# Residual additions of a two-block transformer kernel: matmul results copied to SBUF by ScalarE first, then added by VectorE

## The reference

```python
# first block, two layers
n = rms_norm(h, attn_norm[l])
h = h + mixer(n, ...) @ w_out
h = h + conv_glu_ffn(rms_norm(h, ffn_norm[l]), ...)      # ... @ w_down
# second block, two layers
h = layer_norm(DN_ALPHA * h + token_mixers(h, ...) @ w_out, ln1_g[l], ln1_b[l])
h = layer_norm(DN_ALPHA * h + conv_ffn(h, ...) @ w_down, ln2_g[l], ln2_b[l])
```

## Time and profile before

| | |
|---|---|
| time, median of 3 runs | 2877.43 us (2876.21 to 2878.27) |
| the profiled execution's own time | 2877.43 us |
| its span, first to last instruction | 2875.4 us |
| TensorE busy | 2709.6 us, 94% |
| VectorE busy | 1725.8 us, 60% |
| ScalarE busy | 1005.6 us, 35% |
| GpSimd busy | 1020.5 us, 35% |
| mean granted TensorE clock | 0.964 of full speed |

### The profile page before, as it was taken

One profiled execution on the slowest core, in us unless ns is written; L12 is line 12 of the kernel. 1 busy time (PEld: TensorE's weight loads), 2 busy tenths in 40 slices (PEclk: granted clock), 3 DMA queues, 4 the chain that ended last, 5 costly groups with the idle time before them and its releaser, 6 DMA issues.

```text
span 2875.4 us, 34500 instructions
## 1 busy us (share of the span) xinstructions
PE 2709.6 (94%) x11434; PEld 1997.4 (69%) x11434; DVE 1725.8 (60%) x2250; ACT 1005.6 (35%) x1548; POOL 1020.5 (35%) x383
## 2 busy tenths in 40 slices
PE   8999999999998999999698998999989998899998
PEld 6654788888764678888475455788767644687876
DVE  3645774575486576377559336827634943583682
ACT  3344322232144242232442434323344334432332
POOL 2210344444321244444144123444424411344452
PEclk9997999999998899999899999999999998999999
DMA  4110223232211123223111011222221110122221
GB/s 152 59 45 23 73 95 102 90 103 86 81 52 37 45 94 102 89 95 102 45 54 52 30 39 64 97 93 95 98 71 59 47 44 23 66 95 96 94 99 69
DMA packets 56404, 212.15 MB, mean 74 GB/s; under 512 B 6400, under 2 KB 6656, under 8 KB 56192
## 3 DMA queue, kind: packets, MB, share of 16 engines
q1 hardware_dynamic: 55456, 209.60, 21.6%
q10 hardware_dynamic: 864, 1.44, 0.2%
HBM read 208.92 MB, written 2.10 MB: 73 GB/s over the span
## 4 chain that ended last, share of the span: by engine, by line
PE 75%; DVE 11%; ACT 5%; issue 5%; POOL 3%; DVEq 1%; ACTq 0%; DMA 0%; POOLq 0%; SPq 0%
PE bank_G L499 21%; PE bank_G L501 20%; PE bank_G L500 20%; PE bank_S L1128 4%; POOL wlo L447 3%; PE bank_O L1138 2%; DVE conv_up L751 2%; PE bank_X L1148 2%; DVE mx L2025 1%; PE bank_S L546 1%; PE bank_X L1693 1%; ACT whi L472 1%; DVE prod L771 1%; PE bank_X L820 1%; DVE scores_t L1671 1%
## 5 line engine op out<-in xcount | busy, mean ns | idle before, releaser
L447 POOL TENSOR_TENSOR wlo<-raw,whi 128x1024 fp32r<-128x1024 f32 (+1 forms) x361 | 977.7, 2709 | 1726.6 <-ACT whi L472 1726.6
L499 PE MATMUL bank_G<-n_hi,whi 128*128 128x512 f32 x2392 | 974.8, 408 | 62.5 <-DVE n_lo L606 24.7
L501 PE MATMUL bank_G<-n_hi,wlo 128*128 128x512 f32 x2392 | 942.2, 394 | 0.0
L500 PE MATMUL bank_G<-n_lo,whi 128*128 128x512 f32 x2392 | 942.0, 394 | 0.0
L472 ACT ACTIVATE whi<-raw 128x1024 fp32r<-128x1024 f32 (+1 forms) x363 | 404.3, 1114 | 825.4 <-PE bank_G L501 825.3
L499 PEld LDWEIGHTS bank_G<-n_hi,whi 128*128 128x128 f32 x2392 | 456.4, 191 | 203.4 <-issue 59.1
L501 PEld LDWEIGHTS bank_G<-n_hi,wlo 128*128 128x128 f32 x2392 | 455.3, 190 | 98.7
L500 PEld LDWEIGHTS bank_G<-n_lo,whi 128*128 128x128 f32 x2392 | 456.8, 191 | 95.8 <-issue 7.7
L666 DVE SCALAR_TENSOR_TENSOR h<-h,bank_G 128x512 f32 (+1 forms) x96 | 66.0, 688 | 393.1 <-PE bank_G L501 393.1
L499 PE MATMUL bank_G<-a_hi,whi 128*128 128x512 f32 x704 | 275.3, 391 | 5.8 <-DVE a_lo L773 3.6
L500 PE MATMUL bank_G<-a_lo,whi 128*128 128x512 f32 x704 | 274.0, 389 | 0.0
(11 more groups left out here) (270 smaller groups left out, 2552.2 us busy)
## 6 DMA issues: line engine op xcount, KB each, us to landing
raw<-in_w_mix_in SPq DMA_DIRECT2D x42, 512.0 KB, 3.2
raw<-in_w_out SPq DMA_DIRECT2D x32, 512.0 KB, 3.2
raw<-in_w_hyb_in SPq DMA_DIRECT2D x25, 512.0 KB, 3.2
raw<-in_w_diff_in SPq DMA_DIRECT2D x24, 512.0 KB, 3.2
raw<-in_w_up0a SPq DMA_DIRECT2D x22, 512.0 KB, 3.2
raw<-in_w_up0b SPq DMA_DIRECT2D x22, 512.0 KB, 3.2
raw<-in_w_up1a SPq DMA_DIRECT2D x22, 512.0 KB, 3.2
raw<-in_w_up1b SPq DMA_DIRECT2D x22, 512.0 KB, 3.2
```

Source lines behind the costliest of these rows:

```text
L447: pool.tensor_tensor(b.wlo[:, g.slot, 0:width], b.raw[:, g.slot, 0:width], b.whi[:, g.slot, 0:width], ALU.subtract).then_inc(b.lo_ready, 1)
L499: pe.matmul(out, b.whi[:, g.slot, w], hi[:, k, :], start=(k == 0), stop=False)
L500: pe.matmul(out, b.whi[:, g.slot, w], lo[:, k, :], start=False, stop=False)
L501: mm = pe.matmul(out, b.wlo[:, g.slot, w], hi[:, k, :], start=False, stop=(k == pieces - 1))
```

## The change

ScalarE now empties the bank in the residual groups as well: `products_act` calls `take` (a copy of the bank to `mixed`, a buffer of two 128x512 tiles in SBUF, and behind it `split_hi`) where it had called `split_hi`. VectorE's addition reads `mixed` in the bank's place, waits for `evacuated` in place of `gemm_done`, and signals a new semaphore `resid_done`. The copy into a half of `mixed` waits until the addition two tiles before has read it. Waits on `evacuated` that had meant "h is updated" become waits on `resid_done`, the eight gained copies behind out0 and out1 each wait for their own tile in place of the last, and two waits that ScalarE had at the start of groups, for all of the preceding group to be evacuated, go.

```diff
-def products_act(act, b, name, gain=None):
+def products_act(act, b, name, r0, gain=None):
     g0, tiles = group_tiles(name)
     width = WIDTH[g0]
     if gain:
         for k in range(tiles):
-            split_hi(act, b, Index(g0 + k + 2))
+            wait(act, b.resid_done, r0 + k - 1 if k else max(r0 - 1, 0))
+            take(act, b, Index(g0 + k), b.mixed[:, (g0 + k) % 2, :])
             if k and not name.startswith("out"):
-                act.wait_ge(b.evacuated, g0 + k)
+                act.wait_ge(b.resid_done, r0 + k)
                 gained_hi_act(act, b, gain, k - 1)
 
         for k in range(0 if name.startswith("out") else tiles - 1, tiles):
-            act.wait_ge(b.evacuated, g0 + (tiles if name.startswith("out") else k + 1))
+            act.wait_ge(b.resid_done, r0 + k + 1)
             gained_hi_act(act, b, gain, k)
         return
 
-    for i, g, g_next in pairs(act, g0, tiles - 2):
-        split_hi(act, b, g.after(2), width)
-        split_hi(act, b, g_next.after(2), width)
-    split_hi(act, b, Index(g0 + tiles))
-    split_hi(act, b, Index(g0 + tiles + 1))
+    def one(g, r, w=None):
+        wait(act, b.resid_done, r)
+        take(act, b, g, b.mixed[:, g.slot, :], width=w)
+
+    one(Index(g0), max(r0 - 1, 0))
+    one(Index(g0 + 1), r0)
+    for i, g, g_next in pairs(act, g0 + 2, tiles - 4):
+        one(g, r0 + 1 + 2 * i, width)
+        one(g_next, r0 + 2 + 2 * i, width)
+    one(Index(g0 + tiles - 2), r0 + tiles - 3)
+    one(Index(g0 + tiles - 1), r0 + tiles - 2)
@@ products_dve @@
-    def one(g, h, last=False):
-        dve.wait_ge(b.gemm_done, g.at(1))
-        dve.scalar_tensor_tensor(h, h, float(alpha), b.G[:, g.slot, :], ALU.mult, ALU.add).then_inc(b.evacuated, 1)
+    def one(g, h, r, last=False):
+        dve.wait_ge(b.evacuated, g.at(1))
+        ins = dve.scalar_tensor_tensor(h, h, float(alpha), b.mixed[:, g.slot, :], ALU.mult, ALU.add).then_inc(b.resid_done, 1)
         if stats == "square":
-            dve.wait_ge(b.evacuated, g.at(1))
+            dve.wait_ge(b.resid_done, r)
             link(dve.tensor_tensor(b.sq[:, 0, :], h, h, ALU.mult))
         if last:
             if stats == "sum":
-                dve.wait_ge(b.evacuated, g.at(1))
+                dve.wait_ge(b.resid_done, r)
             dve.sem_inc(b.last_ready, 1)
         elif stats:
-            dve.wait_ge(b.evacuated, g.at(1))
+            dve.wait_ge(b.resid_done, r)
...
@@ ffn_up_act @@
-    if not scaled:
-        act.wait_ge(b.evacuated, g0)
```

More of the change, by code:

```diff
@@ L305, in allocate @@
     b.nlo_ready = sem("nlo_ready")
+    b.resid_done = sem("resid_done")
     b.conv_done = sem("conv_done")
@@ L681, in products_dve @@
                 dve.sem_inc(b.acc_ready, 1)
-            one(Index(g0 + k), b.h[:, k, :], last=k == tiles - 1)
+            one(Index(g0 + k), b.h[:, k, :], RES[name] + k + 1, last=k == tiles - 1)
             if k and not name.startswith("out"):
@@ L691, in products_dve @@
         for s, x in enumerate((g, g_next)):
-            one(x, b.h[:, bass.ds(2 * i + s, 1), :].rearrange("p a t -> p (a t)"))
+            one(x, b.h[:, bass.ds(2 * i + s, 1), :].rearrange("p a t -> p (a t)"), RES[name] + 1 + s + 2 * i)
     link.end(looped // 2)
     if stats:
-        one(Index(g0 + tiles - 2), b.h[:, tiles - 2, :])
+        one(Index(g0 + tiles - 2), b.h[:, tiles - 2, :], RES[name] + tiles - 1)
         dve.sem_inc(b.acc_ready, 1)
-        one(Index(g0 + tiles - 1), b.h[:, tiles - 1, :], last=True)
+        one(Index(g0 + tiles - 1), b.h[:, tiles - 1, :], RES[name] + tiles, last=True)
+RES = {}
+for _n in range(4):
+    RES.update({f"out{_n}": 24 * _n, f"down{_n}a": 24 * _n + 8, f"down{_n}b": 24 * _n + 16})
 def ffn_up_pe(pe, b, name, nlo):
@@ L787, in ffn_act @@
         ffn_up_act(act, b, f"up{f}{tag}", FC * f + HC * half)
-        products_act(act, b, f"down{f}{tag}", gain if half else None)
+        products_act(act, b, f"down{f}{tag}", RES[f"down{f}{tag}"], gain if half else None)
 def ffn_dve(dve, b, link, f, stats, gain=None, nhi=0):
@@ L2245, in _ @@
             hyb_attention_act(act, b)
-            products_act(act, b, "out0", "ffn_norm0")
+            products_act(act, b, "out0", RES["out0"], "ffn_norm0")
             rms_scale_act(act, b, link, 1)
@@ L2252, in _ @@
             diff_attention_act(act, b, link)
-            products_act(act, b, "out1", "ffn_norm1")
+            products_act(act, b, "out1", RES["out1"], "ffn_norm1")
             rms_scale_act(act, b, link, 3)
@@ L2261, in _ @@
                 mixer_act(act, b, link, l, mixw)
-                products_act(act, b, f"out{2 + l}")
+                products_act(act, b, f"out{2 + l}", RES[f"out{2 + l}"])
                 layer_norm_act(act, b, link, 6 + 2 * l, f"ln1_b{l}", 64 + 24 * l, True)
```

## The result

The changed kernel takes 2891.8 us (median of 4 executions, 2888.1 to 2892.9) where the kernel before takes 2876.8 beside it (2872.4 to 2878.3): ratio 1.0053 [1.0037, 1.0069], 15 us slower. A repetition gave 2891.75 against 2876.0, the same ratio. The forecast was 2884.6, 2880.5 to 2891.5: right in direction, less than half of the size. The profiled execution of after takes 2890.4 us, its span 2888.4 at a mean granted clock of 0.961; before it was 2875.4 at 0.964.

A forecast was written before the change was run, and what follows sets the result against it. The prediction saw TensorE bound by its product tiles, plus chains over other engines where it waits. Delays at eight ends and three starts summed to 7.15 us on 2877.4, giving 2884.6, range 2880.5 to 2891.5.

The forecast's parts named there:

- The view of the kernel: Copies inside runs of product tiles cost nothing; only those in chains over other engines that TensorE waits for cost time.
- The direct sum: Delays at group ends and starts, 1.52 + 0.76 + 1.60 + 1.47 + 1.80 = 7.15 us, without any clock term.
- The handover at the ends: Gap from ScalarE's copy to VectorE's operation at group ends, taken as 0.04 us; 0.16 was the upper bound.
- an end of the first kind: Ends of down0b, down1b and down3b, 0.76 us later each; ends of out0 and out1, 0.80 each.
- the ends with a mean: Ends of out2, down2b and out3: POOL's split holds the first centring, 0.49 us later each, 1.47 in all.
- the starts: Third tile of out1, out2 and out3, where TensorE waits for wlo: 0.6 us later each, 1.8 in all.
- TensorE's wait at out0's end: Sign that the forecast is right: this wait grows from 1.67 to about 2.5 us in the profile after.
- a split inside a run: POOL's weight split in out1 had 1.8 us to spare; 1.3 would be left after the copy.
- The order of VectorE and POOL: At the ends VectorE's square still starts before POOL's split, by 0.27 us, or 0.15 with the long handover.
- The rival in which the square loses: At ends of down0b, down1b, out0 and out1 the square waits behind POOL's split: 13.7 us, 2891.1; chance 0.12.
- The clock: Low-clock TensorE stretches behind waits: taken as zero, with the range widened, more upward; one or two stretches are 2 to 4 us.
- A count of low-clock stretches that differs by more than two: Sign that the forecast is wrong, to be read in the profile after.

The follow-up runs named there:

- both direct: Changed kernel, but the first two tiles of the out groups and the last tile before each norm added straight from the bank: 2874.32 us, ratio 0.9993 to before.
- shifted kernels: Changed kernel with two or four extra memsets ahead of the first weight split, shifting it by 1.3 or 2.6 us: 2888.18 and 2889.56 us.
- Halves: Changed kernel with only the last tiles before norms, or only the out groups' first two tiles, added straight from the bank: 2889.16 and 2887.53 us.
- single places: "both direct" with the copy back at block 1's ends, block 2's ends, out2's start or out3's start alone: 2881.62, 2882.49, 2878.62, 2882.97 us.
- bridging: A few unread TensorE products put into the waits that the change lengthens: changed kernel 2888.95 us (1.0044), kernel before 2874.16 us (0.9987).

## Why the forecast was right in direction and wrong in size

**The view of the kernel** held: a copy inside a run is free ("both direct" makes 80 and is not slower), and only the places where ScalarE or VectorE stand directly between two products pay.

**The direct sum** held. Forecast 7.15, bounds 5.4 to 8.5; the trace's gaps give 6.7, the rest apart from the clock +7.2 +- 0.9, and doubling the copy doubles it. Its small errors: the addition takes 0.69, not 0.75; the row that it was taken from has a per-partition scalar (`vec`) where this one has a constant. That is 0.06 too much at five places. The handover at the ends is 0.03 (taken as 0.04). So an end of the first kind costs 0.70 (forecast 0.76 and 0.80), the ends with a mean 0.48 (0.49), the starts 0.62 (0.6). Of the signs that were named, TensorE's wait at out0's end did not go to 2.5 but stayed at 1.67, with the growth in the wait before it; and a split inside a run has 1.07 us to spare, not 1.3.

**The order of VectorE and POOL** was called right: the square starts 0.35 ahead of the split at down0b's end (forecast 0.27) and takes 0.69. The rival in which the square loses gives 2891.1, which is nearly the measured time, and is still wrong: its long squares don't exist, as all 32 take 691 to 695 ns. A number that fits is no evidence for its mechanism.

**The clock** is the step that failed: "I leave it at nothing and widen the range". It is +8.0 +- 1.4 us, as much as the direct sum. Neither reason for leaving it at nothing carried that far. The first was that such a stretch "comes or doesn't come after nearly the same wait", so that longer waits make it only "a little more likely". That holds for the pair of the earlier trace rows, but the start of out2 turned from never to always when its wait went from 1.2 to 1.9. The second was that three executions within 2.1 us meant that the sum evens out. Scatter within a kernel says nothing on a shift of its mean, and three were few: 102 executions reach over 15 us. "A count of low-clock stretches that differs by more than two" was named as a sign against the forecast, and it came: 33 and 36.

**What stays open.** The slow third tiles of out2 and out3 are some 3.2 us of lost time and are explained by the idling ahead of them. For the remaining 4 to 5 us of the clock part no cause is shown. In the two traces of after the largest piece, 4.6 us, lies between down2b's end and out3, partly in a mixer without a copy, and it is gone in the traces of the shifted kernels. Halves and single places each have a clock part whose sum exceeds the whole; bridging lowers both kernels alike; a shift takes off a little. Also unexplained is the rest of "both direct", -2.0 +- 0.9, against which the rests of the four single places add up to 11.8, where the trace's gaps make 5.5 (with 0.12 off at each of the five ends of the first kind); so the parting into clock part and rest is good to a few us, not better.

## What to carry to other kernels

An operation put between a product and its consumer is free inside a pipelined run and costs its full length, plus handover, where the engines take turns: count these places and read one of each kind. Then ask what the longer wait does to TensorE's clock on the products behind it; when a kernel waits for a microsecond or two at many places, such a lengthening can cost as much again, as it did here, and it deserves a term with a positive expectation, not zero. Where a wait can't be removed, a few cheap products on data that are ready anyway can pay for themselves (0.13% here, with 18 of them). 111 of them cost 6 us.

## What the hardware showed that I had not expected

- Low-clock time is worth 0.31 us of span per us over whole executions, but in out2's third tile 0.47: mean clock 0.76 over 7.0 us is 3.4 us at the lower level, and 1.6 were lost. The Trainium skill (TensorE: Matmul & The Clock Gate, Terms) reckons the penalty as this time multiplied by the share of the clock that is withheld, which at 1.2 of 2.4 GHz is half. The tile, where TensorE is the limit, agrees. Over the whole kernel it is less, presumably because much of the low-clock time lies where something else is waited for; no run separates that.
- TensorE idling 1.90 us ahead of the product of 1701.24 was followed by a stretch partly at 1.2 GHz in the traces with this start copied, 1.23 or 1.29 us by none. With extra products that left 0.57 of the wait idle, the stretch did not come.
- A `scalar_tensor_tensor` of 128x512 takes 0.69 with a constant, whether its second tensor comes from the bank (688 ns) or from SBUF (693), and 0.75 with a per-partition scalar. If POOL's split has begun, the SBUF form waits for its end: 1.46 and up to 2.94.
